# A hybrid decoder step on one core: norm for the columns from the diagonals of rows, cached values in more buffers and fewer visits, first scores two by two

## What is computed

```python
def rms_norm(x, g):
    y = xf * lax.rsqrt(jnp.mean(xf * xf, axis=-1, keepdims=True) + RMS_EPS)
...
    xn = rms_norm(x, norm_mix_g)
    q, k, v, hc, gb, gc = _project(xn, w_in)
    parts = [_dilated_prompt(qf, kf, vf, w, d, slopes) for w, d in zip(WINDOWS, DILATIONS)]
    attn_o = _merge_branches(parts)
    u = gc * hc
    conv_o = gb * _short_conv(u_ext, w_conv, t)
    y = _finish(x, attn_o, conv_o, w_out, norm_ffn_g, w_gate, w_up, w_down)
```

## Time and profile before

| | us |
|---|---|
| median of 3 runs | 1224.04 (1223.93 to 1224.21) |
| the profiled execution: its time | 1223.98 |
| its span | 1222.2 |
| PE busy | 1206.4 (99%) |
| DVE, POOL, ACT busy | 604.0, 512.6, 429.3 |
| DMA moved | 174.00 MB, 142 GB/s in the mean |

### The profile page before, as it was taken

The page is one execution under the profiler, slowest core; times in us unless marked ns, Lnnn a source line. Parts: engine busy times, 40 slices in busy tenths (PEclk is TensorE's granted clock), DMA queues, the critical chain, the costliest instruction groups (busy, mean ns, idle before and its releaser), DMA issues.

```text
span 1222.2 us, 22827 instructions
## 1 busy us (share of the span) xinstructions
PE 1206.4 (99%) x9323; PEld 1142.8 (94%) x9323; DVE 604.0 (49%) x1013; ACT 429.3 (35%) x810; POOL 512.6 (42%) x436
## 2 busy tenths in 40 slices
PE   7999999999999999999999999999999999999998
PEld 6998779889877799999999999999999999999998
DVE  6798324315577632479442424341111179756665
ACT  6111120010378811255333333333333444345452
POOL 3346023233144442042897777777777640000020
PEclk9999999999999999999999999999999999999999
DMA  5487656343233142010535455543222485222223
GB/s 212 143 298 239 233 199 272 138 169 128 78 110 104 54 178 70 1 36 36 189 141 191 174 190 174 190 139 122 71 88 71 155 337 220 92 91 95 81 77 107
DMA packets 67800, 174.00 MB, mean 142 GB/s; under 512 B 7088, under 2 KB 24176, under 8 KB 63472
## 3 DMA queue, kind: packets, MB, share of 16 engines
q1 hardware_dynamic: 67552, 172.27, 40.5%
q10 hardware_dynamic: 144, 0.27, 0.1%
HBM read 132.01 MB, written 40.51 MB: 141 GB/s over the span
## 4 chain that ended last, share of the span: by engine, by line
PE 52%; DVE 1%; issue 0%; ACT 0%; DVEq 0%; ACTq 0%
PE ps L1406 11%; PE ps L1408 11%; PE ps L1407 11%; PE ps L1432 6%; PE ps L1433 6%; PE ps L1434 6%; DVE combo_b L1995 0%; DVE w_lo L2391 0%; PE ps L1286 0%; DVE norms L1990 0%; PE ps L1278 0%; PE ps L1306 0%; DVE late L2504 0%; PE ps L1296 0%; DVE raw L2409 0%
## 5 line engine op out<-in xcount | busy, mean ns | idle before, releaser
L1406 PE MATMUL ps<-combo,w_hi 128*128 128x264 f32 x672 | 191.1, 284 | 0.0
L1408 PE MATMUL ps<-combo,w_lo 128*128 128x264 f32 x672 | 190.8, 284 | 0.0
L1407 PE MATMUL ps<-combo,w_hi 128*128 128x264 f32 x672 | 190.4, 283 | 0.0
L944 PE MATMUL ps<-act_hi,w_hi 128*128 128x352 f32 x480 | 157.5, 328 | 8.7 <-DVE act_lo L2000 8.7
L946 PE MATMUL ps<-act_hi,w_lo 128*128 128x352 f32 x480 | 154.6, 322 | 0.0
L945 PE MATMUL ps<-act_lo,w_hi 128*128 128x352 f32 x480 | 154.5, 322 | 0.0
L1432 PE MATMUL ps<-hid,w_hi 128*128 128x264 f32 x536 | 152.7, 285 | 0.0
L1433 PE MATMUL ps<-hid,w_hi 128*128 128x264 f32 x536 | 152.4, 284 | 0.0
L1434 PE MATMUL ps<-hid,w_lo 128*128 128x264 f32 x536 | 152.3, 284 | 0.0
L853 POOL TENSOR_TENSOR w_lo<-w_stage,w_hi 128x512 fp32r<-128x512 f32 (+1 forms) x71 | 99.3, 1399 | 122.5 <-ACT w_hi L1508 122.4
L1408 PEld LDWEIGHTS ps<-combo,w_lo 128*128 128x128 f32 x672 | 126.4, 188 | 0.0
(11 more groups left out here) (427 smaller groups left out, 2993.9 us busy)
## 6 DMA issues: line engine op xcount, KB each, us to landing
w_stage<-in_w SPq DMA_DIRECT2D x61, 512.0 KB, 3.6
resid<-in_state_k SPq DMA_DIRECT2D x8, 1792.0 KB, 10.6
v_buf<-in_state_v SPq DMA_DIRECT2D x14, 1024.0 KB, 6.5
h_d<-evac SPq DMA_DIRECT2D x44, 264.0 KB, 2.1
norms<-in_w SPq DMA_DIRECT2D x22, 512.0 KB, 4.4
t_d<-norms SPq DMA_DIRECT2D x11, 1024.0 KB, 7.5
resid<-in_xT SPq DMA_DIRECT2D x16, 528.0 KB, 7.1
raw<-in_w SPq DMA_DIRECT2D x14, 512.0 KB, 3.8
```

Source lines behind the costliest of these rows:

```text
L944: pe.matmul(out, hi, rhs_hi, start=first, stop=False)
L1406: pe.matmul(out, hi[:, wk], x_hi[:, k, tk], start=(k == 0 and first), stop=False, skip_group_check=not first)
L1407: pe.matmul(out, hi[:, wk], x_lo[:, k, tk], start=False, stop=False, skip_group_check=not first)
L1408: mm = pe.matmul(out, lo[:, wk], x_hi[:, k, tk], start=False, stop=(k == 3), skip_group_check=not first)
```

## The change

`column_sums`, `col_mean` and `col_root` go. In `column_rstd` DVE multiplies each 128 x 128 square of the finished `r_in` with the identity and sums along the row (`tensor_tensor_reduce`), which leaves the diagonal, so the factor of position p in partition p. The wait for `made` moves ahead of it; ACT waits for `col_put` only where it first uses `r_col`. The cached values get two more buffers of four samples, in the room of `early` (which is `pair_hi` and `pair_lo`), and a fifth in two halves; they are worked on behind jobs 3, 11, 18, 22 and 25. Of the first scores, 0 and 1 stand together behind job 34, and 2 and 3 with turn(0) and turn(1) behind part 1 of job 35; ACT copies both turns ahead of the exponentials of step 2, and DVE has conv_out(3, 1) ahead of step 0.

```diff
@@ -212,7 +212,10 @@
         key_bias = resid[:, 8 * ROW:8 * ROW + KEYS + 2 * SAMP]
-        v_ring = [v_buf[:, i, :].rearrange("p (j n) -> p j n", j=4) for i in range(2)]
+        v_ring = [v_buf[:, i, :].rearrange("p (j n) -> p j n", j=4) for i in range(2)] + [
+            early[:, x, 1:3, :].rearrange("p k t -> p (k t)")[:, 0:2048].rearrange("p (j n) -> p j n", j=4) for x in range(2)]
+        v_pair = [early[:, x, 2, 0:1024].rearrange("p (j n) -> p j n", j=2) for x in range(2)]
+        v_room = [tuple(v[:, 2 * x:2 * x + 2, :] for x in range(2)) for v in v_ring] + [tuple(v_pair)]
         s_row = out32[:, :, :].rearrange("p a t -> p (a t)")[:, 0:ROW]
@@ -258,7 +261,7 @@
-        k_ld, v_ld = [sem("k_ld0"), sem("k_ld1")], [sem("v_ld0"), sem("v_ld1")]
+        k_ld, v_ld = [sem("k_ld0"), sem("k_ld1")], [sem(f"v_ld{i}") for i in range(3)]
@@ -275,7 +278,7 @@
-        col_mean, col_root = sem("col_mean"), sem("col_root")
+        col_put = sem("col_put")
@@ -460,9 +463,14 @@
                 b, i = divmod(n, KBLK)
-                if n >= 2:
-                    sp.wait_ge(s_pv, n - 1)
-                sp.dma_start(v_ring[n % 2], state_v[i, :, 4 * b:4 * b + 4, :]).then_inc(v_ld[n % 2], 16)
+                room = VALUE_ROOM[n]
+                if VALUES_GONE[n]:
+                    sp.wait_ge(s_pv, VALUES_GONE[n])
+                if room < 4:
+                    sp.dma_start(v_ring[room], state_v[i, :, 4 * b:4 * b + 4, :]).then_inc(v_ld[min(room, 2)], 16)
+                else:
+                    for x in range(2):
+                        sp.dma_start(v_room[4][x], state_v[i, :, 4 * b + 2 * x:4 * b + 2 * x + 2, :]).then_inc(v_ld[2], 16)
 
@@ -511,26 +519,31 @@
                 unit(16 + n)
-                if n == 1:
+                if n == 0:
+                    sp.wait_ge(val_copied, V_JOBS)
+                    sp.wait_ge(rows_stored[0], 16 * rows_stored_by(QK_JOBS - 4))
+                    sp.wait_ge(rows_stored[1], 16 * rows_stored_by(QK_JOBS - 3))
+                    sp.wait_ge(rows_stored[2], 16 * rows_stored_by(QK_JOBS - 2))
+                    sp.wait_ge(rows_stored[3], 16 * rows_stored_by(QK_JOBS - 1))
                     load_values(2)
                     load_values(3)
+                if n == 1:
                     load_keys(6)
...
                     load_values(5)
+                if n == 3:
+                    load_values(6)
                 if n == 4:
-                    load_values(6)
                     load_values(7)
-                if n == 5:
                     load_values(8)
+                    load_values(9)
                 if n == 6:
-                    load_values(9)
                     load_values(10)
-                if n == 7:
                     load_values(11)
                     load_values(12)
-                if n == 8:
+                if n == 7:
                     load_values(13)
@@ -972,14 +985,6 @@
 
-            def column_sums():
-
-                pe.wait_ge(mean_sq, 2)
-                for tt in range(VT):
-                    m = P if tt < VT - 1 else SAMP
-                    mm = pe.matmul(ps[0:m, 1, tt:tt + 1], ssum[:, P * tt:P * tt + m], ones[:, 0:1], start=True, stop=True)
-                mm.then_inc(ss_done, 1)
-
             for j in range(NC, QK_JOBS):
@@ -991,7 +996,6 @@
                     first_sum(2)
-                    column_sums()
 
@@ -1030,9 +1034,10 @@
                 b, i = divmod(n, KBLK)
-                pe.wait_ge(v_ld[n % 2], 16 * (n // 2 + 1))
+                room = VALUE_ROOM[n]
+                pe.wait_ge(v_ld[min(room, 2)], VALUES_LOADED[n])
                 for j in range(4):
-                    mm = pe.matmul(ps[32 * j:32 * j + 32, 2, :], s_turn[:, i, 32 * j:32 * j + 32], v_ring[n % 2][:, j, :],
+                    mm = pe.matmul(ps[32 * j:32 * j + 32, 2, :], s_turn[:, i, 32 * j:32 * j + 32], v_room[room][j // 2][:, j % 2, :],
                                    start=False, stop=(i == KBLK - 1))
@@ -1214,21 +1219,20 @@
                     sample_channels(1)
-                if cj == 33:
-                    scores(0)
-
+
+            scores(0)
+            scores(1)
             conv_bank_free(CONV_JOBS - 1)
             last_conv_part(0)
-            scores(1)
             last_conv_part(1)
...
             pe.wait_ge(c_used, 12)
+            pe.wait_ge(b_used, 11)
             scores(2)
+            scores(3)
             turn(0)
+            turn(1)
             last_conv_part(2)
-            pe.wait_ge(b_used, 11)
-            scores(3)
-            turn(1)
             last_conv_part(3)
@@ -1534,9 +1538,6 @@
                 take_root(c)
-            act.wait_ge(col_mean, 1)
-            act.activation(r_col[:, :], r_col[:, :], ACT.Sqrt).then_inc(col_root, 1)
-            act.wait_ge(col_mean, 2)
             for j in range(QK_JOBS):
@@ -1545,6 +1546,7 @@
 
+            act.wait_ge(col_put, VT)
             for j in range(QK_JOBS, QK_JOBS + V_JOBS):
@@ -1640,8 +1642,8 @@
                     turned_copies(b)
+                    turned_copies(b + 1)
                     exponentials(b + 2)
-                    turned_copies(b + 1)
                     exponentials(b + 3)
@@ -2014,11 +2016,14 @@
 
-                dve.wait_ge(col_root, 1)
-                dve.reciprocal(r_col[:, :], r_col[:, :]).then_inc(col_mean, 1)
+                for tt in range(VT):
+                    m = P if tt < VT - 1 else SAMP
+                    at = slice(P * tt, P * tt + m)
+                    dve.tensor_tensor_reduce(work[0:m, at], r_in[0:m, at], ident[0:m, 0:m], 1.0, 0.0, ALU.mult, ALU.add,
+                                             r_col[0:m, tt:tt + 1]).then_inc(col_put, 1)
+                dve.wait_ge(col_put, VT)
                 chain(dve.tensor_tensor(r_in2, r_in, r_in, ALU.mult))
 
-            chain(dve.memset(r_col[:, :], 1.0))
             for k in range(KT):
@@ -2054,16 +2059,12 @@
             mean_square(2)
-            dve.wait_ge(ss_done, NC + 1)
-            dve.tensor_scalar(r_col[:, 0:VT - 1], ps[:, 1, 0:VT - 1], 1.0 / D, EPS, ALU.mult, ALU.add)
-            dve.tensor_scalar(r_col[0:SAMP, VT - 1:VT], ps[0:SAMP, 1, VT - 1:VT], 1.0 / D, EPS, ALU.mult, ALU.add
-                              ).then_inc(col_mean, 1)
             first_rstd(1)
...
             row_out(2)
+            dve.wait_ge(made, 2)
             column_rstd()
-            dve.wait_ge(made, 2)
             dve.wait_ge(consts_in, 32)
@@ -2316,12 +2317,12 @@
             conv_out(3, 0)
+            conv_out(3, 1)
             step_scores(0)
-            conv_out(3, 1)
             step_scores(1)
             reciprocals(0)
+            reciprocals(1)
             step_scores(2)
-            reciprocals(1)
             turned_copies(0)
@@ -2690,7 +2691,10 @@
 LATE_SCORES_BEHIND = {3: (4, 5), 11: (6, 7)}
-VALUES_BEHIND = {3: (0, 1), 7: (2, 3), 11: (4, 5), 13: (6,), 18: (7, 8), 21: (9, 10), 24: (11, 12), 26: (13,)}
+VALUES_BEHIND = {3: (0, 1, 2, 3), 11: (4, 5, 6), 18: (7, 8, 9), 22: (10, 11, 12), 25: (13,)}
+VALUE_ROOM = [0, 1, 2, 3, 0, 1, 2, 0, 1, 4, 0, 1, 4, 0]
+VALUES_LOADED = [16, 16, 32, 32, 32, 32, 48, 48, 48, 80, 64, 64, 112, 80]
+VALUES_GONE = [0, 0, 0, 0, 1, 2, 3, 5, 6, 7, 8, 9, 10, 11]
 
```

## The result

| | before | after |
|---|---|---|
| median (11 runs each, in turn on one chip) | 1224.21 us (1223.88 to 1224.89) | 1227.67 us (1226.26 to 1228.16) |
| ratio after / before | | 1.0025, interval 1.0017 to 1.0033 |
| the profiled execution: time, span | 1223.98, 1222.2 | 1228.16, 1226.4 |

The change makes the kernel 3.5 us slower. The forecast was 1225.4 us with "no difference" as the likeliest case, and the time lies 0.5 us above its range. Those of before form one.

A forecast was written before the change was run, and what follows sets the result against it. PE's own stream was taken as the bound (busy 1206.4 of 1222.2 us). The terms -0.26 - 1.0 + 2.7 = +1.4 us, on a median of 1224.04, gave 1225.4 us; range 1222.4 to 1227.2.

The forecast's parts named there:

- What bounds the kernel: Whole kernel: PE's own stream, busy 1206.4 of 1222.2 us; only a shorter stream or new PE waits count.
- Rival A: Column sums and first scores: waits don't bite, matmul time counts in full, -3.3 us, 1220.7 us; chance 0.09.
- Part 1: Column sums moved to VectorE: 1.93 us leave PE, a 1.67 us stall ahead of job 9 returns; -0.26 us.
- Part 2: Cached values: three visits fewer at 0.32 us each, loads fitting by 0.5 us; -1.0 us.
- Part 3: First scores side by side: stalls of 1.45 us ahead of scores(1), 1.2 ahead of scores(3); 2.7 us slower.
- The sum: Whole kernel: column sums, cached values and first scores, -0.26 - 1.0 + 2.7 = +1.4 us, so 1225.4 us.
- Rival B: First scores: two gaps let PE's clock fall to 1.2 GHz, 1.3 us each; 1226.7 to 1228.1 us; chance 0.11.

The follow-up runs named there:

- part 1 alone: Kernel before with only the column sums made by nine VectorE reduces; cached values and first scores as before: 1223.88 us.
- parts12_reordered: parts12 with VectorE's row_out(3) ahead of the nine reduces and r_in2 behind row_out(5): 1221.44 us, ratio 0.9978.
- reordered_all_parts: Changed kernel with VectorE's row_out(3) ahead of the nine reduces and r_in2 behind row_out(5), gaps at the first scores unfilled: 1224.27 us.
- first_gap_doubled: Changed kernel, but VectorE makes head_bias(0, 0) a second time ahead of step_scores(0), so PE idles longer ahead of scores(1): 1229.41 us.
- filled and unfilled pair: first_gap_doubled with and without unread matmuls, fifteen ahead of scores(1) and six ahead of scores(3): 1227.54 us filled, 1229.41 us unfilled.
- parts12: Kernel before with column sums on VectorE and cached values in more buffers and five visits; first scores as before: 1223.64 us.

## Why the prediction was wrong, step by step

- **What bounds the kernel**: right. Every difference of half a microsecond that the traces show lies in PE's stream or its waits. Rival A (the waits don't bite) was wrong: both waits are there.
- **Part 1**, -0.26: measured -0.2 (within its uncertainty of 1 us), with the stall named and the reduces at 0.21. The agreement is partly luck. From start to start the column sums were worth 2.03 (forecast 1.93) and the stall took 1.94 of it (forecast 1.67), so that in the trace of part 1 alone job 9 gains only 0.1 on the start's shift. Job 9's slower restart (0.08) and the slower spacing behind it (0.16) take 0.24, and 0.35 come back at sample_turn(0). There ScalarE's exponential waits for VectorE's `s_neg`, 2.07 us before and 1.71 in part 1 alone, and PE stands behind it in a hidden wait that the list of waits of before did not show.
- **Part 2**, -1.0: the term that was mis-sized. Three visits fewer at 0.32 were there, but I took the spacing of the tile matmuls behind them for a constant. With all its gains in the trace the part is worth -0.5 (from -2.27 to -2.77 us against before between sample_turn(0) and scores(0) in parts12_reordered). The loads fitted by as little as I said: in one of the kernels they did not, 0.5 us.
- **Part 3**, +2.7: right in the two waits (1.36 and 1.15, forecast 1.45 and 1.2) and in the sum at full clock: 3.0 alone, 2.5 to 2.7 on the mended parts 1 and 2 (1223.95 or, filled, 1224.15, less 1221.44).
- **The sum** of the measured terms at full clock is -0.2 - 0.5 + 2.8 = +2.1, so 1226.3, which is the lower group. That is 0.9 above the forecast and inside its range: 0.5 of it is part 2, 0.2 that before measured 1224.21 here and not 1224.04, the rest parts 1 and 3.
- **The rivals** are where it failed. Rival B had the mechanism, the place and the price: 1.3 us for each fall, measured 1.5. That the measured 1227.67 lies in its 1226.7 to 1228.1 is partly luck: for one fall B says 1226.7, and it reaches 1228.1 with a second fall that the second gap alone never caused; here one fall came on top of a sum 0.9 higher. I gave B 0.11 because the gaps were short beside the 8 us of the start. That compared with the only idle stretch of more than 0.7 us in the trace of before and took it for a threshold; nothing in that trace said how short a gap must be to be harmless. The step that failed is this one: the path of part 3 was summed at full clock, with the fall at nothing, and seven of eleven executions had it, at 1.5 us. On the other chip, where two of eleven had it, the same kernel's median of 1226.19 lies inside the forecast's range; so that the median fell outside is chance in part, and the two groups are what the forecast missed in both. The question of what an unseen state costs was asked, and then weighed by the absence of a row. The sign that "what would show it" gives for B, tile matmuls spaced near 0.3 behind the first scores, is what the trace shows.

## What to carry to other kernels

Before tile work is taken from between two instructions that depend on each other over another engine, count what the gap costs twice: its length, and the chance that TensorE's clock is at 1.2 GHz for some microseconds after it. If such a gap must be, unread matmuls in it took the second cost away here and cost 0.2 us at most (1224.15 against the lower group's 1223.95, 1226.3 against 1226.15). When work is moved from the bound engine to a helper, place it behind the helper's results that the bound engine waits for next: the same nine reduces brought 0.1 us up to job 9 in one order and 2.0 in the other. The best kernel of this study (parts 1 and 2 with VectorE's order mended, first scores as before) runs in 1221.44 us, 0.22% under before.

## What the runs showed of the hardware

- TensorE's granted clock fell to half after 1.36 us of idleness between two stretches of full work, about 1 us after the work had begun again (0.9 to 1.3), and stayed there for 3.4 us in each of the three traces that caught it (after, reordered_all_parts, and first_gap_doubled behind 2.63 us of idleness); in other executions of the same kernel it did not fall at all. The Trainium skill ("TensorE: Matmul & The Clock Gate", section "What's actually happening") says that a gate sets the array's clock by how busy the engine has been of late. The filled and unfilled pair agrees; that the same program is caught in one execution and not in the next is shown here by the groups.
- Behind some visits of small matmuls (`128*32` in the rows), back-to-back matmuls of 352 columns were spaced 0.160 to 0.163 instead of 0.159 us for 10 us and more, at a granted clock of 1.00. In parts12 it was so behind visits of 5.8, 2.7 and 1.0 us (jobs 11, 22, 25) and not behind the longest (7.7 us, job 3). Near job 9 it came in some traces and not in others. The runs show where it happens and what it costs (0.2 us each time), not why.
- The first matmuls of an execution are spaced 0.29 us, until 10.8 us in one profile and until 16.0 in another. With that and the waits between them, all that follows is shifted by -0.2 to +1.9 us between profiles, by 0.7 between two of the same kernel.
